# Filling TensorE's pause behind each norm with repeated products of constants

## What is computed

```python
def rms_norm(x, g):
    xf = x.astype(jnp.float32)
    y = xf * lax.rsqrt(jnp.mean(xf * xf, axis=-1, keepdims=True) + NORM_EPS)
    return (y * g.astype(jnp.float32)).astype(x.dtype)

def adaln(x, g, shift, scale):
    return rms_norm_2(x, g) * (1 + scale[:, None, :]) + shift[:, None, :]

def swiglu(h, w_in, w_out):
    a, b = jnp.split(h @ w_in, 2, axis=-1)
    return (jax.nn.silu(a) * b) @ w_out
```

## Time and profile before

| | |
|---|---|
| median of 3 runs | 4082.64 us (4080.52 to 4090.14) |
| profiled execution, its own time | 4088.53 us |
| its span, first to last instruction | 4086.7 us |
| mean granted TensorE clock | 0.951 |
| TensorE busy | 3799.0 us (93%) |
| VectorE busy | 2690.6 us (66%) |
| ScalarE busy | 1816.0 us (44%) |
| GpSimd busy | 1459.3 us (36%) |
| DMA | 664.39 MB, 163 GB/s |

### The profile page before, as it was taken

How to read it: one execution, slowest core, us unless ns; L and a number is a source line. 1 busy time by engine, 2 the same in 40 slices (tenths; PEclk the granted TensorE clock), 3 DMA queues, 4 the chain that set the end, 5 groups by cost and what they waited for, 6 DMA issues and landing times.

```text
span 4086.7 us, 69652 instructions
## 1 busy us (share of the span) xinstructions
PE 3799.0 (93%) x29090; PEld 3511.6 (86%) x29090; DVE 2690.6 (66%) x4831; ACT 1816.0 (44%) x3088; POOL 1459.3 (36%) x848
## 2 busy tenths in 40 slices
PE   7999998999899889899999989989999999999899
PEld 6779997799899767699998959989879998767699
DVE  4568776688677765577777677677677734665542
ACT  3344444544454432254546535444454544432343
POOL 2024432344344420144454413444224444320244
PEclk9899998999999989899999989999999999979899
DMA  5126652376566310056664406756427553300152
GB/s 206 63 78 253 262 199 91 124 270 256 183 240 258 110 42 1 16 217 260 237 261 159 147 32 237 268 213 260 172 100 272 221 194 132 104 27 1 47 182 108
DMA packets 63689, 664.39 MB, mean 163 GB/s; under 512 B 7056, under 2 KB 7568, under 8 KB 7952
## 3 DMA queue, kind: packets, MB, share of 16 engines
q1 hardware_dynamic: 63376, 659.94, 43.1%
HBM read 658.86 MB, written 1.05 MB: 161 GB/s over the span
## 4 chain that ended last, share of the span: by engine, by line
PE 72%; DVE 19%; ACT 5%; issue 2%; POOL 1%; DMA 0%; SPq 0%; DVEq 0%; ACTq 0%; POOLq 0%
PE pb L275 70%; DVE wp L228 5%; DVE ada_acc L240 3%; ACT wp L266 3%; PE pb L282 2%; DVE wk L240 2%; DVE wk L228 2%; DVE sq L228 2%; DVE sq L240 1%; DVE hT L240 1%; ACT wk L266 1%; ACT sq L266 1%; DVE hx L240 1%; DVE rsb L228 1%; POOL sq L228 0%
## 5 line engine op out<-in xcount | busy, mean ns | idle before, releaser
L275 PE MATMUL pb<-hx,wp 128*128 128x256 f32 x15744 | 1989.5, 287 | 96.2 <-DVE hx L240 40.4
L275 PEld LDWEIGHTS pb<-hx,wp 128*128 128x128 f32 x15744 | 1951.6, 195 | 116.7 <-issue 103.5
L228 POOL TENSOR_TENSOR wp<-ring,wp 128x512 fp32r<-128x512 f32 (+1 forms) x596 | 1244.8, 2105 | 1877.4 <-ACT wp L266 1835.8
L228 DVE TENSOR_TENSOR wp<-ring,wp 128x1024 fp32r<-128x1024 f32 (+1 forms) x670 | 818.2, 1241 | 357.1 <-ACT wp L266 355.6
L266 ACT ACTIVATE wp<-ring 128x1024 fp32r<-128x1024 f32 x936 | 938.6, 1046 | 232.5 <-PE pb L275 225.3
L275 PE MATMUL pb<-ex,wp 128*128 128x256 f32 x5856 | 757.5, 287 | 23.6 <-DVE ex L228 23.6
L275 PEld LDWEIGHTS pb<-ex,wp 128*128 128x128 f32 x5856 | 729.6, 195 | 25.2 <-issue 19.7
L240 DVE SCALAR_TENSOR_TENSOR ada_acc<-ring,cact,ada_acc 128x384 f32<-128x384 f32 x576 | 530.0, 984 | 44.2 <-ACT ada_acc L266 44.2
L275 PE MATMUL pb<-wk 128*128 128x128 f32 (+8 forms) x3136 | 401.5, 294 | 13.8 <-ACT wk L266 6.4
L275 PEld LDWEIGHTS pb<-wk 128*128 128x128 f32 (+4 forms) x3136 | 299.5, 174 | 110.1 <-issue 41.8
L228 DVE TENSOR_TENSOR sq<-sq,pb 128x256 f32<-128x256 f32 (+1 forms) x360 | 161.1, 448 | 322.2 <-ACT sq L266 272.2
(11 more groups left out here) (179 smaller groups left out, 2895.9 us busy)
## 6 DMA issues: line engine op xcount, KB each, us to landing
ring<-weights SPq DMA_DIRECT2D x385, 1536.0 KB, 6.6
ring<-weights SPq DMA_DIRECT2D x41, 1024.0 KB, 4.8
ring<-weights SPq DMA_DIRECT2D x4, 512.0 KB, 10.5
cst<-consts SPq DMA_DIRECT2D x1, 2032.0 KB, 12.1
ring<-weights SPq DMA_DIRECT2D x1, 1280.0 KB, 5.9
prm<-params SPq DMA_DIRECT2D x1, 1258.0 KB, 7.7
ring<-weights SPq DMA_DIRECT2D x1, 1152.0 KB, 5.1
xT<-xT_in SPq DMA_DIRECT2D x1, 1024.0 KB, 5.1
```

Of the source, the lines that this page charges most:

```text
L228: return self.real.tensor_tensor(out, a, b, op) if self.real else Uncounted()
L275: return self.real.matmul(out, l, r, start=start, stop=stop, skip_group_check=skip)
```

## The change

Between the sums of squares and the first product of the next stage TensorE repeats products of the tile of ones with the identity, plain float32, 128 x 128 by 128 columns, into the PSUM tile that the next product is about to overwrite. It is done 17 times ahead of: `ck` in nsa; `l_gate` in both ple; `l_k` in moba and swa; products(0) in all eight ffn; the dt product in mamba. Ahead of `l_r` in both rwkv it is done 34 times. Two places aren't behind a norm: 17 ahead of `l_q` in moba and 17 ahead of `l_out` in nsa. The moe stages have none. That makes 340 repeated products. They wait for nothing but their PSUM bank. No other engine's program is changed.

```diff
+    def repeated_pe(e, ps, n):
+
+        for _ in range(n):
+            e.mm(ps[:, 0:128], ones[:, 0:128], ident, True, True, skip=True)
+
+    BEHIND_NORM = 17
+
-    def lin_pe(e, lin, x, ready, freed, behind=lambda m: None):
+    def lin_pe(e, lin, x, ready, freed, behind=lambda m: None, ahead=0):
...
                 ps = bk.take(e, key, (freed, key))
+                if m == 0:
+                    repeated_pe(e, ps, ahead)
...
             if u == 0:
                 pair = g.pieces[u][0:2]
+                if cw is None:
+                    repeated_pe(e, ps, BEHIND_NORM)
...
-                lin_pe(e, l_win[name], in_hx, lambda c: (x_lo, (st, "h", c)), v_out)
+                lin_pe(e, l_win[name], in_hx, lambda c: (x_lo, (st, "h", c)), v_out,
+                       ahead=BEHIND_NORM if name == "ck" else 0)
...
-            lin_pe(e, l_out, in_hx, lambda c: (x_lo, (st, "o", c)), x_new)
+            lin_pe(e, l_out, in_hx, lambda c: (x_lo, (st, "o", c)), x_new, ahead=BEHIND_NORM)
...
-            lin_pe(e, l_k, x_kv, lambda c: (x_lo, (st, t_kv, c)), v_out)
-            lin_pe(e, l_q, x_q, lambda c: (x_lo, (st, t_q, c)), v_out)
+            lin_pe(e, l_k, x_kv, lambda c: (x_lo, (st, t_kv, c)), v_out, ahead=BEHIND_NORM)
+            lin_pe(e, l_q, x_q, lambda c: (x_lo, (st, t_q, c)), v_out, ahead=BEHIND_NORM if t_q != t_kv else 0)
...
-            lin_pe(e, l_gate, in_hx, lambda c: (x_lo, (st, "h", c)), a_out)
+            lin_pe(e, l_gate, in_hx, lambda c: (x_lo, (st, "h", c)), a_out, ahead=BEHIND_NORM)
...
             ps = bk.take(e, (st, "dt"), (v_out, (st, "dt")))
+            repeated_pe(e, ps, BEHIND_NORM)
             e.wait_ge(*v_step[st, "dt weights"])
...
-            lin_pe(e, l_r, in_hx, lambda c: (x_lo, (st, "mix", 0, c)), a_out)
+            lin_pe(e, l_r, in_hx, lambda c: (x_lo, (st, "mix", 0, c)), a_out, ahead=2 * BEHIND_NORM)
```

More of the change, by code:

```diff
@@ L1077, in att_stats @@
         return wk[:, off + 2 * NB * 384 + n % NB * 8:off + 2 * NB * 384 + (n % NB + 1) * 8]
-    def repeated_pe(e, ps, n):
-        for _ in range(n):
-            e.mm(ps[:, 0:128], ones[:, 0:128], ident, True, True, skip=True)
     BEFORE_SCORES, BEFORE_TURN, BEFORE_VALUES = {0: 8, 5: 3, 6: 2}, 10, 4
```

## The result

The changed kernel took 4089.41 us (median of 20 runs, 4082.68 to 4107.97) against 4082.88 us (20 runs, 4078.25 to 4090.14) for the kernel before. The ratio is 1.0022, with a 95% interval of 1.0013 to 1.0031: slower by 0.2%, clear of the noise, though under the 0.3% that I had called measurable. I had forecast 5 us less. The runs fall in two groups, eleven from 4082.7 to 4090.3 and nine from 4097.8 to 4108.0; before they lie in one. The profiled execution, 4102.56 us with a span of 4100.8, is of the upper group, so its excess is larger than the median's.

The account below looks back on a forecast made before the run. TensorE was taken to bound the kernel only where no VectorE work of the chain follows. Gains of 8.0 us less 2.9 given back left 5.1, so 4077.5 us from a median of 4082.64, range 4064 to 4090.

Parts of the forecast that it names:

- What bounds the kernel: Whole kernel: TensorE holds 72% of the chain, VectorE 19%; shortening TensorE pays only where no VectorE piece of that chain follows.
- the worth of the fill in the six ada stages: Feed-forward with ada: 0 saved, since VectorE's chain sets down(0), 15.9 us after the first product, and TensorE only idles longer.
- What is added: Ahead of the filled products: 340 repeats costed at nothing; 17 take 4.06 us inside waits, any overrun under 1 us.
- The loss at the second pause: TensorE's idle time ahead of the ada product: clock falls in four of six stages instead of two, 2.9 us lost, at most 5.8.
- The gains: All filled stages: 8.0 us saved in sum, mostly nsa's `l_out` 2.2, moba's `l_q` 2.4, ple 1.2 and mamba 1.1.
- the line in the prediction on mamba: Mamba's fill ahead of dt: 1.1 us gained, bounds 0 and 3.4, as `l_conv` begins with 2 us of slow clock left.
- The clock falls by luck in as many other places: Part of an 8% rival that the change doesn't do what it says: nothing moves, 4082.6 us, a few us either side.
- small gain: Whole kernel, the main forecast at 50%: 4077.5 us, with its own range 4071 to 4083.
- Given back: Rival, 25%: all six ada stages fall, clock falls again ahead of `l_q`, VectorE eats mamba's part; about 4084 us.
- Full price: Rival, 12%: every slow microsecond over 17 places counts, 40.2 us saved, giving 4042 us.
- repeats on the path: Rival, 5%: at the lower clock 17 repeats take 7.6 us and delay first products, 24 us slower, 4107 us.

Follow-up runs that it names:

- the first trace: The changed kernel's profiled execution, compared with one traced execution of the kernel before: 4102.56 us, with mamba at 317.7 against 304.1 us.
- the two later traces: The changed kernel, unaltered, traced two more times: 4094.23 and 4085.25 us, with mamba at 311.2 us in both.
- the two pauses held: 7 repeats ahead of each ada feed-forward stage's first ada product, 17 ahead of mamba's first head: 4068.56 us on the changed kernel, 4072.57 on the kernel before.
- the heads filled: The changed kernel plus 17 repeats ahead of the first head's product in mamba: 4079.06 us, ratio 0.9991 to the kernel before.
- the ada fill: The changed kernel plus 7 repeats ahead of the first ada product in each feed-forward stage with ada: 4068.56 us, ratio 0.9967 to the kernel before.

## Why the prediction was wrong, point by point

- **What bounds the kernel, and the worth of the fill in the six ada stages: right.** The chain through VectorE stands, down(0) starts 15.86 us after the first product, products(0) and (1) end with 1.61 us to spare, and the fill saves nothing there (4080.08 without it against 4089.41 with it).
- **What is added: right.** 17 repeats took 3.96 us (4.06 forecast), 34 took 7.75, and the 17 begun at the lower clock 5.48 in moba's `l_k` and 5.17 in stage 6. In stage 6 they overran: the first product came 4.68 us after the norm's logarithm instead of 4.08, and the 0.6 us were taken up by the waits below, as the prediction has it.
- **The loss at the second pause: mis-sized.** I put two further stages at 1.45 us, 2.9. In the first trace four further fell (six in all): 6.6 us, above even my bound of 5.8, which had one stretch a stage. In the two later traces four and three fell, for 4.7 and 3.3 us, so my count of four was fair. What I had too low is stage 9, which is slow twice as long in all three (down(0) 5.49 us) and loses 2.65 us alone. What the Trainium skill says of pauses between groups ("TensorE: Matmul & The Clock Gate", section "A second HAM failure mode"), that they are enough for the clock to swing, agrees with the first trace in all six stages and with the others only in part.
- **The gains: right in sum, by luck.** 8.0 us forecast; in the first trace nsa 3.7 (2.5 forecast), ple 0.6 (1.2), moba 1.1 (2.4; the clock fell again, as its lower bound allowed), swa 1.3 (0), ffn without ada 0.2 (0.2), with 1.1 in the moe stages that I had not counted, together 8.0. The same stages gave 7.2 and 12.2 us in the two later traces. Against these stand mamba and rwkv, which lost 2.0 us instead of gaining 0.6 (in the later traces it lost 1.1 and gained 1.6). With the two pauses held, the whole change was worth about 4.
- **The step that failed** is the line in the prediction on mamba and, with it, on everything behind the first products: "`l_conv` begins 6 us in with 2 us of slow clock left: 1.1 us, bounds 0 and 3.4". The gain did not come, since the first head waits for VectorE and began 172.95 us after the norm against 172.80. And mamba lost 13.6 us in the first trace and 7.1 in each of the two later ones, in its loop over heads, a term that I had put at nothing. I had costed the stages only where the change puts something, and everything else at zero difference. "The clock falls by luck in as many other places" stood in a rival at 8% and "a few us to either side", while the trace already showed 20 us of slow clock in the loop over heads, behind a wait of 4.3 us. Had I priced its bounds by the rows (never slow, 0.5 x 20 = 10 us less; twice as long, 10 more), the range would have had to reach to about 4100.
- **The range** of 4064 to 4090 holds the median of 4089.4 at its very edge; the sign was wrong. (The small gain's own range doesn't follow from its bounds, which give 4069 to 4084 and not 4071 to 4083.) "Given back", at 25%, came nearest in what happened: in the first trace all six stages fell, the clock fell again ahead of `l_q`, and mamba's VectorE ate its part. It too has nothing on the loop over heads, and its 4084 is 5 us short. "Full price" and "repeats on the path" were rightly small: no run of any kernel here came under 4067 us, and only stage 6 and moba's `l_k` had a first product held up by the repeats, stage 6's by 0.6 us.

What stays open: why the loop over heads comes back to the full clock after 6, 20, 34 or 48 us. The time of the fall orders twelve of the fourteen traces, but what in the loop brings the clock back wasn't tried. Nor was it settled which of several places parts the changed kernel's two groups of runs, or how the 6.5 us between the medians, as against the 14 us between the traces, divide over the stages.

## What to carry to other kernels

Filling a pause of TensorE paid here only where TensorE's own work set the next wait. In most stages VectorE's did, and the fill moved the idle time to a second pause, where the clock fell in work that did count. Look for the pause *after which* TensorE bounds the kernel and fill that one (7 repeats in each of six places and 17 in one gave 11 us on their own; the 340 gave about 4 more beside them, and a loss without them). Where a fill lengthens a later pause, fill that one too. In this kernel an added microsecond changed a later stage by 13 to 19 us; compare stage by stage and over many runs and traces before a small gain or loss is put down to an edit.

## What was not expected of the hardware

A loop in which TensorE was busy without a gap (10.00 of each 10 us) stayed at the lower clock for up to 48 us, and the same loop held the upper clock to its end once it began with it. In the changed kernel's first trace, repeats of small constant products held the clock wherever the next product came within 0.6 us of them, and it fell where 1.9 (moba) or 2.4 us (rwkv) were left. That is no rule: with the heads filled, and with the ada fill, it held over the same 2.4 us ahead of stage 7. And 0.9 us of added work made a kernel 5 us faster in the median and a stage of it 19 us shorter than in the first trace of the changed kernel, 13 shorter than in the other two.
